# A PEER stage on one Trainium2 core: the u rows' products taken as 512 columns, two halves summed afterwards, and one of two one-hot tables made by GpSimd

## The reference, cut to what matters

```python
def peer_mixer(h, w_q, keys_1, keys_2, u_tab, v_tab):
    ...
    v1, i1 = lax.top_k(s1, PEER_TOPK)
    v2, i2 = lax.top_k(s2, PEER_TOPK)
    ...
    experts = (e1 * PEER_N_KEYS + e2).reshape(t, PEER_HEADS * PEER_TOPK)
    gates = jax.nn.softmax(sc, axis=-1).reshape(t, PEER_HEADS * PEER_TOPK)
    def expert_block(args):
        hb, eb, gb = args
        a = jax.nn.gelu(jnp.einsum('td,ted->te', hb, u_tab[eb]).astype(jnp.float32), approximate=False)
        w = (gb * a).astype(hb.dtype)
        return jnp.einsum('te,ted->td', w, v_tab[eb])
```

## Time and profile before

| | us |
|---|---|
| median of 3 executions | 2494.4 (2493.58 to 2494.79) |
| the profiled execution's own time | 2495.44 |
| its span, first to last instruction | 2493.6 |
| u part of PEER, keys with list work | 1701 to 1868.6 |
| u part, keys with one-hot groups | 1868.6 to 2107.6 |
| u part, last keys | 2107.6 to 2129.9 |
| v part | 2129.9 to 2480 |

### The profile page before, as it was taken

How to read it: one execution, slowest core, us unless ns; L and a number is a source line. 1 busy time by engine, 2 the same in 40 slices (tenths; PEclk the granted TensorE clock), 3 DMA queues, 4 the chain that set the end, 5 groups by cost and what they waited for, 6 DMA issues and landing times. The chain is left out here.

```text
span 2493.6 us, 34777 instructions
## 1 busy us (share of the span) xinstructions
PE 2336.3 (94%) x14382; PEld 1589.2 (64%) x14382; DVE 1212.6 (49%) x2476; ACT 724.5 (29%) x1267; POOL 15.1 (1%) x22
## 2 busy tenths in 40 slices
PE   8999999999998888888988889999999999999998
PEld 6787678962232223222322247889999999888887
DVE  4677985621111111111111126158887776788887
ACT  2135566420000000000000013224454444455554
POOL 1000000000000000000000000000000000000000
PEclk9999999999999999999999989899999999999999
DMA  5375555768999999999999973215775555877875
GB/s 163 118 221 171 174 169 171 251 276 361 427 426 427 427 427 426 427 427 426 427 427 427 426 283 114 89 51 166 229 223 173 178 178 179 251 242 240 243 242 162
DMA packets 205452, 677.52 MB, mean 272 GB/s; under 512 B 15072, under 2 KB 137200, under 8 KB 180336
## 3 DMA queue, kind: packets, MB, share of 16 engines
q1 hardware_dynamic: 205296, 675.30, 72.9%
HBM read 657.40 MB, written 17.83 MB: 271 GB/s over the span
## 5 line engine op out<-in xcount | busy, mean ns | idle before, releaser
L1112 PE MATMUL ps<-ring,tokens 128*34 128x512 f32 x1264 | 279.4, 593 | 25.7 <-DMA ring<-in_w_up 18.3
L2156 PE MATMUL ps<-m_hi,row_hi 128*128 128x256 f32 x1024 | 256.4, 288 | 0.8 <-ACT peer_s L2222 0.8
L2156 PE MATMUL ps<-m_lo,row_hi 128*128 128x256 f32 x1024 | 250.7, 283 | 0.0
L605 PE MATMUL ps<-u,ring 128*128 128x272 f32 x1024 | 244.7, 395 | 3.0 <-DVE ring L423 3.0
L605 PEld LDWEIGHTS ps<-u,ring 128*128 128x128 f32 x1024 | 191.5, 190 | 46.2 <-issue 7.2
L1112 PEld LDWEIGHTS ps<-ring,tokens 128*34 128x34 f32 x1264 | 71.6, 112 | 229.8 <-issue 178.9
L1112 PE MATMUL ps<-extra_early,tokens 128*34 128x512 f32 x752 | 197.5, 674 | 19.9 <-DMA extra_early<-in_w_up 12.3
L1247 DVE TENSOR_SCALAR spread<-ps,slot_at 98x272 fp32r<-98x272 f32 x16 | 8.0, 500 | 396.3 <-PE ps L1098 396.3
L2156 PEld LDWEIGHTS ps<-m_hi,row_hi 128*128 128x128 f32 x1024 | 195.7, 191 | 1.6 <-issue 1.0
L2156 PEld LDWEIGHTS ps<-m_lo,row_hi 128*128 128x128 f32 x1024 | 196.1, 191 | 0.0
L1135 PE MATMUL ps<-ring,first_room 128*34 128x512 f32 x752 | 174.3, 613 | 21.9 <-DVE first_room L1265 10.5
(11 more groups left out here) (430 smaller groups left out, 3179.9 us busy)
## 6 DMA issues: line engine op xcount, KB each, us to landing
ring<-in_w_up SPq DMA_DIRECT2D x47, 2048.0 KB, 23.3
ring<-in_w_down SPq DMA_DIRECT2D x47, 2048.0 KB, 24.2
ring<-in_w_gate SPq DMA_DIRECT2D x32, 2048.0 KB, 22.6
extra_early<-in_w_gate SPq DMA_DIRECT2D x31, 2048.0 KB, 21.4
ring<-in_w_in SPq DMA_DIRECT2D x36, 1024.0 KB, 5.4
extra_early<-in_w_up SPq DMA_DIRECT2D x16, 2048.0 KB, 24.6
extra_early<-in_w_down SPq DMA_DIRECT2D x16, 2048.0 KB, 25.7
rows<-in_peer_u SPq DMA_DIRECT2D x64, 512.0 KB, 3.9
```

Of the source, the lines that this page charges most:

```text
L605: last = pe.matmul(bank[:, 0:T], wt[:, k, c:c + P], s.u[:, k, :], start=k == 0, stop=k == KT - 1)
L1112: last = pe.matmul(ps[HALF * j:HALF * j + CAP, 2 * c + u % 2, :], s.tokens[:, 2 * (u // 2) + k, CAP * i:CAP * i + CAP], rows[k][:, 1024 * ...
L2156: pe.matmul(out, hi[:, P * k:P * k + P], m[:, k, :], start=k == 0 and m is s.m2_hi, stop=False)
```

## The change

TensorE's 16 matmuls of the upper part become 8. `m2_hi` and `m2_lo` now lie side by side for each slice in one tile `m2_parts` (slice, part, token), so that one matmul of 512 columns multiplies the row's upper part by both. The bank then holds two halves: the upper part times `m2_hi` (to which the 8 matmuls of the lower part are added, as before), and the upper part times `m2_lo`. They have to be summed before Gelu. ScalarE copies the second half into a new tile `half_sum` (one buffer), VectorE adds it to the first half, into `held` (`sum_halves`), and ScalarE makes Gelu in place, one key later (`gelu_of(i - 1)`).

The one-hot table of the second index is taken off VectorE: GpSimd makes it, four instructions a group, one a token. TensorE waits for both tables.

```diff
+            def sum_halves(i):
+                dve.wait_ge(half_out, i + 1)
+                if i >= HELD:
+                    dve.wait_ge(kept[i % HELD], 16 * (i // HELD))
+                dve.tensor_tensor(s.held[:, i % HELD, :], s.half_sum[:, :], s.ps[:, i % 2, 0:SEQ], ALU.add).then_inc(summed, 1)
...
-                        dve.tensor_scalar(h1[:, t, :], s.iota[:, 0:KEYS], e1[:, k:k + 1], gate[:, k:k + 1],
-                                          ALU.is_equal, ALU.mult)
-                    dve.tensor_tensor(h2, s.iota[:, 0:KEYS].unsqueeze(1).to_broadcast([P, TOKENS, KEYS]),
-                                      e2[:, at].unsqueeze(2).to_broadcast([P, TOKENS, KEYS]), ALU.is_equal)\
-                       .then_inc(hot, 1)
+                        last = dve.tensor_scalar(h1[:, t, :], s.iota[:, 0:KEYS], e1[:, k:k + 1], gate[:, k:k + 1],
+                                                 ALU.is_equal, ALU.mult)
+                        if t == TOKENS - 1:
+                            last.then_inc(hot, 1)
...
             for i in range(KEYS):
                 pace.key = i
+                if i >= 2:
+                    sum_halves(i - 2)
                 while room > 0.0:
...
+            sum_halves(KEYS - 2)
             rest(KEYS)
+            sum_halves(KEYS - 1)
             rest(KEYS + 1)
             weigh(2)
...
+        @block.gpsimd
+        def _(pool):
+            pool.wait_ge(turned_out, BATCHES * QT)
+            for g in range(groups):
+                if g >= 2:
+                    pool.wait_ge(product, g - 1)
+                for t in range(TOKENS):
+                    k = TOKENS * g + t
+                    last = pool.tensor_scalar(hot_buffers(g)[1][:, t, :], s.iota[:, 0:KEYS], e2[:, k:k + 1], None, ALU.is_equal)
+                last.then_inc(hot_second, 1)
...
             def spread_weights(g):
                 pe.wait_ge(hot, g + 1)
+                pe.wait_ge(hot_second, g + 1)
...
                 pe.wait_ge(hi_done, i + 1)
                 if i >= 2:
-                    pe.wait_ge(gelu, i - 1)
-                out, hi, lo = s.ps[:, i % 2, 0:SEQ], s.row_hi[:, i % 2, :], s.row_lo[:, i % 2, :]
+                    pe.wait_ge(summed, i - 1)
+                out, hi, lo = s.ps[:, i % 2, :], s.row_hi[:, i % 2, :], s.row_lo[:, i % 2, :]
                 for k in range(KT):
-                    for m in (s.m2_hi, s.m2_lo):
-                        pe.matmul(out, hi[:, P * k:P * k + P], m[:, k, :], start=k == 0 and m is s.m2_hi, stop=False)
+                    pe.matmul(out, hi[:, P * k:P * k + P], s.m2_parts[:, k, :, :].rearrange("p a t -> p (a t)"),
+                              start=k == 0, stop=False, skip_group_check=True)
                 pe.wait_ge(lo_done, i + 1)
...
+            def gelu_of(i):
+                act.wait_ge(summed, i + 1)
+                act.activation(s.held[:, i % HELD, :], s.held[:, i % HELD, :], ACT.Gelu).then_inc(gelu, 1)
...
                 act.wait_ge(hidden, i + 1)
-                if i >= HELD:
-                    act.wait_ge(kept[i % HELD], 16 * (i // HELD))
-                act.activation(s.held[:, i % HELD, :], s.ps[:, i % 2, 0:SEQ], ACT.Gelu).then_inc(gelu, 1)
+                if i:
+                    act.wait_ge(summed, i)
+                act.activation(s.half_sum[:, :], s.ps[:, i % 2, SEQ:2 * SEQ], ACT.Copy).then_inc(half_out, 1)
                 upper(i + 2)
+                if i:
+                    gelu_of(i - 1)
```

More of the change, by code:

```diff
@@ L1953, in peer @@
              "m2_lo", "hi", "lo", "hidden", "gelu", "hot", "product", "spread", "weighted", "act_hi", "act_lo", "used", "early", "y_ready",
-             "y_act", "y_dve", "y_turned", "added", "squares", "total", "std", "scaled", "out")
+             "y_act", "y_dve", "y_turned", "added", "squares", "total", "std", "scaled", "out", "half", "summed", "hot_second")
     (query, query_out, scores, scores_out, shifted, exped, lists, turned, turned_out, m2_hi, m2_lo, hi_done, lo_done, hidden,
      gelu, hot, product, spread, weighted, act_hi, act_lo, used, early_in, y_ready, y_act, y_dve, y_turned, added, squares, total, std,
-     scaled, out_done) = (s.sem(f"peer_{k}") for k in names)
+     scaled, out_done, half_out, summed, hot_second) = (s.sem(f"peer_{k}") for k in names)
     row_in = [s.sem(f"peer_row_in{q}") for q in range(ROWS)]
@@ L2151, in u_products @@
                 if i >= 2:
-                    pe.wait_ge(gelu, i - 1)
-                out, hi, lo = s.ps[:, i % 2, 0:SEQ], s.row_hi[:, i % 2, :], s.row_lo[:, i % 2, :]
+                    pe.wait_ge(summed, i - 1)
+                out, hi, lo = s.ps[:, i % 2, :], s.row_hi[:, i % 2, :], s.row_lo[:, i % 2, :]
                 for k in range(KT):
-                    for m in (s.m2_hi, s.m2_lo):
-                        pe.matmul(out, hi[:, P * k:P * k + P], m[:, k, :], start=k == 0 and m is s.m2_hi, stop=False)
+                    pe.matmul(out, hi[:, P * k:P * k + P], s.m2_parts[:, k, :, :].rearrange("p a t -> p (a t)"),
+                              start=k == 0, stop=False, skip_group_check=True)
                 pe.wait_ge(lo_done, i + 1)
                 for k in range(KT):
-                    last = pe.matmul(out, lo[:, P * k:P * k + P], s.m2_hi[:, k, :], start=False, stop=k == KT - 1)
+                    last = pe.matmul(out[:, 0:SEQ], lo[:, P * k:P * k + P], s.m2_hi[:, k, :], start=False, stop=k == KT - 1,
+                                     skip_group_check=True)
                 last.then_inc(hidden, 1)
@@ L2273, in _ @@
                         store_weights(g)
+            gelu_of(KEYS - 1)
             for j in range(2, KEYS):
```

10 lines of the change are left out of this document (5 added, 5 removed).

## The result

The changed kernel takes 2497.6 us in the median of 17 runs (2494.9 to 2501.8), the kernel before 2493.6 (2492.5 to 2495.4): a ratio of 1.0017, 95% interval 1.0010 to 1.0023. It is slower by 4 us where I forecast 6 to 7 us faster. The profiled execution spans 2496.3 us against 2493.6.

The account below looks back on a forecast made before the run. The prediction took TensorE's own instructions to bound the u part. Its terms, -14.1 + 3.2 + 2.0 + 1.7 = -7.2 us, led to 2487 us, 0.3% faster, with a range from 2481 to 2508.

Parts of the forecast that it names:

- What bounds the kernel: In the u part TensorE's own instructions are the time; VectorE has only 29.2 us of rest in keys with list work.
- TensorE's gain: Eight 512-column matmuls replace 16 of 256 in each of 128 keys: 0.11 us less a key, 14.1 us gained.
- The later Gelu's loads: In keys without a one-hot group, row loads queued behind the later Gelu's write land late: 3.2 us lost (0 to 28).
- the loop: Over two keys, landing, `upper`, Gelu to load, landing take 5.62 us: 2.81 a key against TensorE's 2.77.
- VectorE in the list stretch: In keys with list work, the added sums make `rest` late in runs of long pieces: 2 us lost (0 to 6).
- GpSimd, 0: In one-hot keys, GpSimd's four instructions at 0.33 us each take 1.3 of 3.65 us: no loss if it works alone.
- Into the v part: At the v part's start, the last Gelu ends 2.05 us after its key rather than 0.4, uncovered: 1.7 us lost.
- Blocking: Rival, one-hot keys: VectorE and GpSimd hold each other up, so the kernel ends slower, middle values 2508 us; chance 0.25.
- The list stretch eats the gain: Rival: late loads, `rest`s and sums add up, list keys stay at 2.90 to 2.95 us, 2494 us; chance 0.18.

Follow-up runs that it names:

- two runs with new prices: Changed kernel with list work dealt so every second key gets a long piece, 2498.8 us; with row load before write and v-part and last-Gelu reordering too, 2490.1 us.
- the halves: Changed kernel with each of VectorE's twelve long list pieces cut into two of half the heads: 2496.1 us, ratio 1.0011 to the kernel before.
- the prices that are the durations: Changed kernel, list work dealt by traced durations, long pieces halved, row load before write, last six Gelus first, VectorE's v-part order: 2488.3 us; with whole pieces 2489.8.
- Two edits of order: Changed kernel with the last six Gelus ahead of the wait for the next products, and VectorE's lower parts ahead of weighings at the v part's start: 2490.6 us.
- all of it together: Changed kernel, row load before write, last six Gelus first, VectorE's v-part order, ScalarE copying both halves, sums on GpSimd, both tables on VectorE: 2490.0 us.

## Why the prediction was wrong

- **What bounds the kernel**: right, TensorE in both stretches, and right that VectorE's 29 us of rest in the list stretch are where the change hits.
- **TensorE's gain, -14.1**: mis-sized, -10.4. A key went from 2.88 to 2.79, not 2.77 (65 keys x 0.09), and with a group by 0.07 (63 keys). I took 0.226 for a joined matmul from the v part; here eight take 1.84 us, 0.230, and 1.93 in a key behind a one-hot group. The kernel before has an addition there too, 1.99 for the 16 (1956.26 to 1958.25) against 1.92; what it comes from wasn't tried.
- **The later Gelu's loads, +3.2**: the loop is in the chain as written, 2.78 a key at 3.77 of landing. Taking it away gave 1.4 us in the changed kernel (1.0 to 2.5 by the spread of the profiles). Between the two runs with new prices 3.9 us less were lost, though these differ in the order of the v part and the last Gelus too, which touch no key with list work. The size depends on what else is late.
- **VectorE in the list stretch, +2.0**: mis-sized; of the 6.4 us lost 5.0 stayed when no load was late. I counted 1.5 us missing in each run of six long pieces and let `rest` be 1 late for free. The trace has three keys of 3.7 to 3.8 in one of the runs and two in the other, 1.0 lost each, and small losses in the batch's 256-column pieces. No dealing of the same work cured it: the halves and the first set of prices moved the loss between keys, and the prices that are the durations left 3.6 us of it. From start to start `rest` and sum take 1.14 + 0.34 = 1.48 us, which leaves 1.31 of 2.79 for lists, 69 us in the 53 keys that have them. Their work is 156.7 busy, less 57 x 1.48 and 3 for the first tables, also 69 us (I had put 71 in an expectation): nothing is to spare. My average, 2.79 against 2.77, had said so, and I priced it as if only the long pieces counted. The two terms together were forecast at 5.2 and measured 6.4.
- **GpSimd, 0**: right in the sum, wrong in the price. I bounded an instruction by 0.24 and 0.62 us and took 0.33; it takes 0.60 alone and 1.46 beside `rest`, 0.83 in the mean. Below 3.69 us a key this is free, and moving the table there is worth as little.
- **Into the v part, +1.7**: this step failed, and it is the largest miss: 6.6 us with the last keys. The last Gelu did end about 2.1 us after its key (2129.76 against 2127.6). But I let the lateness pass through at its own size, and misread the row: the 0.61 us were not a wait for the returned values but for `act_lo`, which VectorE made late behind `weigh(3)` and `rest(130)`. For the first returned column TensorE had 1.0 us to spare. The last write then went out 2.1 us later, counted from the first v product (2.70 us behind it, before 0.61), and from that write to the weighing of the first returned column it took 4.37 us (2130.32 to 2134.69), before 2.76 (2130.65 to 2133.41). Both together, less what TensorE had to spare, are the new wait of 2.54. Why the return took longer wasn't tried. The 0.61 became 1.53, and after both TensorE ran eight matmuls at half clock, 1.6 us more: 2.54 + 0.92 + 1.57 = 5.0 of the 5.1 us. The remaining 1.5 are the last keys, where the new sum stands behind an early column's return. Two edits of order took 1.1 + 4.3 = 5.4 us of it back.
- **The rivals.** Blocking (0.25) didn't occur where I put it: VectorE's scalar instructions grew from 343 to 346 ns in the median, 358 in the mean, and `rest` not at all; it was GpSimd that was held up, and nearly always by `rest` alone: an instruction of GpSimd beside it lasts 1.46 us, beside the new sum 0.60 and beside the first table's 0.69. *The list stretch eats the gain* (0.18, 2494) described the stretch well, 6.4 lost of 5.2 gained, and missed the rest. The sum as measured, -10.4 + 6.4 + 1.5 + 5.1 = +2.6 us, is the difference of the spans, 2.7, and its 9.8 us from the forecast's -7.2 are 3.7 of TensorE's gain, 1.2 of the list stretch and 4.9 of the entry. The medians say 4.0: the profiled execution of the kernel before lies 1.9 us above its median (2495.44 against 2493.58), that of the changed kernel 0.4 (2498.02 against 2497.61).

## What to carry to other kernels

When new work brings an engine that is off the path close to the bound's pace over a stretch (here VectorE's 156.7 us busy where TensorE alone needs 162.6), expect a loss in every run of keys that asks it for more than its share, and take its average in the durations of the trace, not in the planner's prices. A producer that ends later at a change of phase can cost more than its lateness, here 6.6 us for 1.7: follow each engine's in-order queue through the first two items of the next phase, read what the wait that is already there is for, and look for waits that leave TensorE idle, since its clock may fall behind them. Here edits of order alone took the changed kernel from 2497.6 to 2490.6 us, more than the change itself moved it.

## What the hardware showed that I had not expected

- GpSimd's comparison with a scalar by pointer, 128 columns: 592 to 1536 ns, median 605, and a two-input add of 256 columns 724 ns at the least; VectorE takes 343 and 417 for the same shapes.

```profile
L2086 POOL TENSOR_SCALAR hot<-iota,lists_t x256: 592/605/1536, 1862.8 to 2099.1; 128x128 f32<-128x128 f32 x128
```

- Contention went mostly against GpSimd. Of its 256 comparisons the 62 that overlap `rest` alone (two inputs from SBUF) last 1464 ns in the median, the 62 that overlap the new sum alone (one input from PSUM) 596. The rows show one that starts 0.21 us after a `rest` and ends 0.46 after it, while `rest` keeps its length. Only GpSimd's two-input adds held VectorE back, by up to 0.54 us (1760 against 1225 ns).

```profile
1957.13 1.21 DVE L1988 TENSOR_TENSOR row_lo<-rows,row_hi 128x1024 fp32r<-128x1024 f32 x1
...
1957.34 1.46 POOL L2086 TENSOR_SCALAR hot<-iota,lists_t 128x128 f32<-128x128 f32 x1
```

- At the v part's start TensorE's waits of 2.54 and 1.53 us, and in the run with the last six Gelus first of 0.71 and 1.49, were followed by the lower clock for 3.4 us, in some other runs for 6.8. It stayed at 1.00 with one wait of 0.67, with 0.63 and 1.09 (all of it together), and with 1.19 and 0.69 six us apart (the halves at prices that are the durations).
